# Three experts with 64 slots and two products per weight tile, placed by token count

## What is computed

```python
def moe_swiglu(h, router, w_gate, w_up, w_down):
    probs = softmax(ht @ router)                    # 256 tokens x 8 experts
    vals, idx = top_k(probs, 2); wts = vals / sum(vals)
    gates = ...                                     # token x expert, two non-zero per token
    for e in range(8):
        out = out + gates[:, e:e + 1] * swiglu(ht, w_gate[e], w_up[e], w_down[e])
# swiglu(h) = (silu(h @ w_gate) * (h @ w_up)) @ w_down; 1024 -> 2048 -> 1024
```

## Time and profile before

| | us |
|---|---|
| median of 3 runs | 1329.01 |
| lowest, highest | 1328.97, 1330.6 |
| span of the profiled execution | 1327.3 |
| TensorE busy in it | 1291.5 (97%) |
| TensorE weight loads | 1074.6 (81%) |
| VectorE busy | 931.9 (70%) |
| ScalarE busy | 835.5 (63%) |
| moved by DMA | 341.68 MB, 257 GB/s |

### The profile page before, as it was taken

One profiled execution on the slowest core, in us unless ns is written; L12 is line 12 of the kernel. 1 busy time (PEld: TensorE's weight loads), 2 busy tenths in 40 slices (PEclk: granted clock), 3 DMA queues, 4 the chain that ended last, 5 costly groups with the idle time before them and its releaser, 6 DMA issues.

```text
span 1327.3 us, 16327 instructions
## 1 busy us (share of the span) xinstructions
PE 1291.5 (97%) x6201; PEld 1074.6 (81%) x6201; DVE 931.9 (70%) x906; ACT 835.5 (63%) x906; POOL 49.6 (4%) x52
## 2 busy tenths in 40 slices
PE   7999999999999999999999999999999998999998
PEld 6888888888887888888888888878778876788887
DVE  4685555446768888888888888898876664645542
ACT  5646444346866878777787878877587655644431
POOL 4001000000005000000000000002010000000000
PEclk9999999999999999999999999999999999999999
DMA  9647755544228999999999999999864341555540
GB/s 313 235 142 271 245 177 172 181 147 149 80 95 323 422 377 414 346 422 358 408 353 410 359 408 365 396 378 380 318 224 167 118 159 64 189 187 174 180 159 32
DMA packets 90233, 341.68 MB, mean 257 GB/s; under 512 B 6267, under 2 KB 14160, under 8 KB 66512
## 3 DMA queue, kind: packets, MB, share of 16 engines
q1 hardware_dynamic: 87200, 330.15, 66.6%
q0 software_dynamic: 2816, 10.67, 2.3%
q10 hardware_dynamic: 160, 0.07, 0.0%
HBM read 333.53 MB, written 11.01 MB: 260 GB/s over the span
## 4 chain that ended last, share of the span: by engine, by line
PE 92%; DVE 4%; ACT 3%; issue 1%; DMA 0%; ACTq 0%; DVEq 0%
PE bank L1704 29%; PE bank L1706 28%; PE bank L1705 28%; DVE w_lo L365 1%; PE bank L2056 1%; PE bank L1816 1%; PE bank L1799 1%; PE bank L1843 1%; ACT w_hi L360 1%; PE bank L2049 0%; DVE x L1076 0%; PE bank L1989 0%; ACT mem_tmp L651 0%; ACT xT_hi L594 0%; DMA gain_rows<-in_norm_mix 0%
## 5 line engine op out<-in xcount | busy, mean ns | idle before, releaser
L365 DVE TENSOR_TENSOR w_lo<-raw,w_hi 128x2048 fp32r<-128x2048 f32 (+3 forms) x246 | 549.3, 2246 | 223.5 <-ACT w_hi L360 222.5
L360 ACT ACTIVATE w_hi<-raw 128x2048 fp32r<-128x2048 f32 (+3 forms) x246 | 460.9, 1883 | 209.6 <-PE bank L1706 197.9
L1704 PE MATMUL bank<-w_hi,xT_hi 128*128 128x512 f32 (+2 forms) x672 | 256.5, 382 | 3.8 <-DVE xT_lo L1048 1.9
L1706 PE MATMUL bank<-w_hi,xT_lo 128*128 128x512 f32 (+2 forms) x672 | 253.4, 377 | 0.0
L1705 PE MATMUL bank<-w_lo,xT_hi 128*128 128x512 f32 (+2 forms) x672 | 253.3, 377 | 0.0
L1704 PE MATMUL bank<-w_hi,gT_hi 128*128 128x512 f32 x512 | 201.5, 394 | 2.8 <-DVE gT_lo L1520 1.5
L1706 PE MATMUL bank<-w_hi,gT_lo 128*128 128x512 f32 x512 | 200.2, 391 | 0.0
L1705 PE MATMUL bank<-w_lo,gT_hi 128*128 128x512 f32 x512 | 199.8, 390 | 0.0
L365 DVE TENSOR_TENSOR w_lo<-raw_beside,w_hi 128x2048 fp32r<-128x2048 f32 x64 | 145.3, 2288 | 8.5 <-ACT w_hi L360 8.4
L1704 PEld LDWEIGHTS bank<-w_hi,xT_hi 128*128 128x128 f32 x672 | 126.8, 189 | 27.8 <-issue 3.7
L360 ACT ACTIVATE w_hi<-raw_beside 128x2048 fp32r<-128x2048 f32 x64 | 122.1, 1917 | 39.5 <-PE bank L1706 38.4
(11 more groups left out here) (381 smaller groups left out, 1340.7 us busy)
## 6 DMA issues: line engine op xcount, KB each, us to landing
raw<-in_moe_w_gate SPq DMA_DIRECT2D x48, 1024.0 KB, 6.0
raw<-in_moe_w_up SPq DMA_DIRECT2D x48, 1024.0 KB, 7.3
raw_beside<-in_moe_w_down SPq DMA_DIRECT2D x32, 1024.0 KB, 9.3
raw<-in_moe_w_down SPq DMA_DIRECT2D x32, 1024.0 KB, 7.7
raw<-in_w_gate_up SPq DMA_DIRECT2D x22, 1024.0 KB, 5.1
raw_beside<-in_moe_w_gate SPq DMA_DIRECT2D x16, 1024.0 KB, 6.5
raw_beside<-in_moe_w_up SPq DMA_DIRECT2D x16, 1024.0 KB, 6.1
raw<-in_ffn_w_gate SPq DMA_DIRECT2D x11, 1024.0 KB, 5.2
```

Source lines behind the costliest of these rows:

```text
L360: nc.scalar.activation(w_hi[:, slot, :n], raw_of(i, stream)[:, :n], ACT.Copy).then_inc(stream.high, 1)
L365: nc.vector.tensor_tensor(w_lo[:, slot, :n], raw_of(i, stream)[:, :n], w_hi[:, slot, :n].bitcast(F32), ALU.subtract).then_inc(stream.low, 1)
L1704: mm(dst, a_hi, b_hi, start=start, stop=False)
L1706: return mm(dst, a_lo, b_hi, start=False, stop=stop)
```

## The change

Experts 1 to 7 are run in an order by their token count: with the counts ranked, places 2, 4 and 6 go to the three lightest, places 1, 3, 5 and 7 to the others; expert 0 stays first. VectorE computes places, first slots and the order in `positions`, inside the first expert, behind low part 3, and `rows_of_choices` comes behind low part 4 instead of ahead of the first expert. SyncE's loop over experts is written out, and it reads the expert of each place from `order` into a register, by which the weights are addressed.

A light place has 64 slots. The high parts of its 64 rows and their low parts stand side by side as the 128 columns of one stationary tile, so one weight tile needs two products, by its high and by its low part (`both`). The two halves of a result have to be added. For gate and up TensorE does it and turns at the same time: ScalarE copies the bank to memory, and a plain float32 product with the constant `fold` (128x64) gives the sum, transposed (`fold_quarter`); silu and the product by up follow on the folded data. For down VectorE adds the halves. More than 64 tokens in a light place, or 128 in another, lead to the second pass.

The other experts keep three products. In the loop, the first two chunks of a gate now start with banks 2 and 3 for both chunks, ahead of the wait for `y`. One loop body now holds two experts.

```diff
+                def both(dst, tokens, wh, wl, start, stop):
+                    mm(dst, tokens, wh, start=start, stop=False)
+                    return mm(dst, tokens, wl, start=False, stop=stop)
+                def fold_quarter(v, b, quarter):
+                    columns = columns_of(v, quarter, 2)
+                    for k in range(4):
+                        at_ = (quarter % 2 * 4 + k) * LIGHT
+                        ins = mm(bank[b][:, at_:at_ + LIGHT], columns[:, k // 2, k % 2, :], fold, start=True, stop=True)
+                    return ins
```

VectorE, light expert and first expert:

```diff
+                def light(e, i, n_high):
+                    for c in range(EXPERT_CHUNKS):
+                        if c == 15:
+                            light_product(e, i, 0)
+                            light_low(e, 0)
+                        split_low(MOE0 + c + AHEAD, e, W1)
+                        if c == 15:
+                            light_product(e, i, 1)
+                        if c == 16:
+                            light_low(e, 1)
+                        if c in (17, 18):
+                            rows_low(n_high + c - 17, 6 + c - 17, c - 17)
+                    dve.wait_ge(sem("light_copied"), y_copied(i))
+                    dve.wait_ge(sem("moe_rows_stored"), 16 + 16 * e)
+                    for half in range(2):
+                        cols = slice(half * HALF, (half + 1) * HALF)
+                        ins = V.tensor_tensor(M["y"][:LIGHT, cols], bank[half][:LIGHT, :], y_low[:, cols], ALU.add)
+                    ins.then_inc(sem("moe_y"), 1)
+                def expert(e, h, n_high, rows_low, first=False):
                     for c in range(EXPERT_CHUNKS):
                         if c == 14:
+                            expert_act(e, h, 0)
                         split_low(MOE0 + c + AHEAD, e, W1)
+                        if first and c == 0:
+                            positions()
+                        if first and c == 1:
+                            rows_of_choices()
...
                 below_best()
-                rows_of_choices()
                 dve.wait_ge(sem("loaded_moe_g"), 16)
```

ScalarE, light expert:

```diff
+                def light(e, i, number):
+                    for c in range(EXPERT_CHUNKS):
+                        split_high(MOE0 + c + AHEAD, e, W1)
+                        if c in (8, 9):
+                            light_gate(e, number, 2 * (c - 8))
+                            light_gate(e, number, 2 * (c - 8) + 1)
+                        if c == 14:
+                            light_silu(i)
+                            for quarter in range(QUARTERS):
+                                light_up(e, i, quarter)
+                        if c in (15, 16):
+                            light_high(e, c - 15)
+                        if c in (17, 18):
+                            rows_high(number + c - 17, 6 + c - 17, c - 17)
```

TensorE, the gate of an expert in the loop, and the middle of a light one:

```diff
+                def gate(e, product, y_read):
+                    first_two = [(k, weights(W1, MOE0 + k, e)) for k in range(2)]
+                    for quarter in (2, 3):
+                        for k, (wh, wl) in first_two:
+                            product(quarter, k, wh, wl, quarter)
+                    pe.wait_ge(sem("moe_y"), y_read)
...
+                def light(e, i, number):
...
+                    pe.wait_ge(sem("light_copied"), gate_copied(i))
+                    for quarter in range(QUARTERS):
+                        ins = fold_quarter(M["e_act"], 2 + quarter // 2, quarter)
+                    ins.then_inc(sem("light_in_psum"), 1)
+                    last_two = [(k, weights(W1, MOE0 + KD + k, e)) for k in (KD - 2, KD - 1)]
```

SyncE:

```diff
+                for p in range(E):
+                    if p == 1:
+                        sp.wait_ge(sem("moe_planned"), 2)
+                    e = sp.value_load(order[0:1, p:p + 1], min_val=0, max_val=E - 1) if p else 0
                     for c in range(EXPERT_CHUNKS):
+                        load_expert(c, p, p == 0, *expert_chunk(A, e, c, p == E - 1))
                         if c == 13:
+                            store_rows(p)
+                        if c == 14 and p < E - 1:
+                            load_rows(p + 1)
```

More of the change, by code:

```diff
@@ L416, in returned, with over_job, over_heavy, heavy_of_pair @@
             return M["back"][:, at, :] if at < 2 * T - 1 else M["moe_g"][:, :]
[L418 to L422, removed]
-            return FIRST_OVER - OVER_JOBS * E + OVER_JOBS * e
+        def over_job(e):
+            return FIRST_OVER - OVER_JOBS * E + OVER_JOBS * e
+        def over_heavy(e):
+            return e - PAIRS
+        def heavy_of_pair(i):
+            return 1 + 2 * i, 1 + i, FIRST_PAIR + PAIR_JOBS * i
+        def light_of_pair(i):
+            return 2 + 2 * i, FIRST_PAIR + TURNED_JOBS + PAIR_JOBS * i
+        SLOTS_AT = [LIGHT if 0 < p < E - 1 and p % 2 == 0 else P for p in range(E)]
+        FIRST_SLOT = [sum(SLOTS_AT[:p]) for p in range(E)]
+        def gate_copied(i):
+            return QUARTERS + 9 * i
+        def up_copied(i, quarter):
+            return QUARTERS + 1 + quarter + 9 * i
+        def y_copied(i):
+            return 9 + 9 * i
+        def gate_turned(i):
+            return 1 + 6 * i
+        def light_up_done(i, quarter):
+            return 2 + quarter + 6 * i
+        def up_turned(i, j):
+            return 5 + j + 6 * i
+        def gated(e, j):
+            return 1 + j + QUARTERS * e
+        def act_high(e, j):
+            return 3 + j + QUARTERS * e
+        def act_known(e, j):
+            return 1 + 2 * j + QUARTERS * e
+        def act_low(e, j):
+            return 2 + 2 * j + QUARTERS * e
         def per_feature(c, n):
@@ L531, in _ @@
                 pool.wait_ge(W1.high, start_of["ffn1_up"] + 4)
-                for e in range(1, E):
-                    small(slots_in[e * P:(e + 1) * P, :], A["shape_blank"], "blank")
+                for p in range(1, E):
+                    at_, n = FIRST_SLOT[p], SLOTS_AT[p]
+                    small(slots_in[at_:at_ + n, :], A["shape_blank"][:n, :], "blank")
                 pool.wait_ge(sem("mla_heads_ready"), 1)
@@ L2086, in expert, with first_expert @@
+                def expert(e, h, number):
+                    pe.wait_ge(sem("moe_drained"), number)
+                    gate(e, product, 1 + e)
+                    pe.wait_ge(sem("moe_act_done"), QUARTERS * e)
+                    rest_of_expert(e, h, number)
+                def first_expert():
+                    pe.wait_ge(sem("moe_drained"), GATHER_JOBS - 1)
                     for k in range(KD):
-                        if first and k == KD // 2:
-                            pe.wait_ge(sem("moe_drained"), number)
```

303 lines of the change are left out of this document (215 added, 88 removed).

## The result

The changed kernel takes 1338.99 us (1337.59 to 1341.67) against 1329.8 (1328.97 to 1331.05) for the kernel before in the same measurement: a ratio of 1.0065, 95% interval 1.0044 to 1.0086. It is slower, by 0.65%. 1314.8 was forecast, over 1303 to 1330. The profiled span is 1335.4 us against 1327.3.

A forecast was written before the change was run, and what follows sets the result against it. TensorE was taken to bound the kernel, with VectorE 8.5 us behind per expert and setting the pace of the lights. The sum was 1329.0 - 20.8 (lights) + 0.8 + 5.8 (first expert) = 1314.8 us, range 1303 to 1330.

The forecast's parts named there:

- first expert: Earlier first product, 1.3 us less, against late low parts 4 and 5: net +0.8 us; plus a 5.8 us stall.
- first light and its heavy: A light expert costs 61.0 us instead of 68.4, and the heavy one behind fills the ring again: 7.4 us less.
- third light and last expert: After the third light the last expert waits for the result before any product, starting at 63.7 us: gains 6.0 us.
- The product step: One 128x512 product on TensorE takes 0.2267 us from start to start; 288 products make 65.3 us of an expert.
- Rival C: Slower by the scatter wait alone, if SyncE is released after about 463 us: some 1334 to 1340 us; chance 0.09.
- The lead of the loads: Chunks landed or under way for about 9 us cover a light's transfers: nothing taken, up to 4 us per light.
- The walk: Light expert followed from the preceding heavy expert's last product: VectorE sets the pace, equivalent start of the next at 61.0 us.
- Rival B: Transfers set a light expert's pace, 65 to 68 us; gains 0.4 to 3.4 each, 1325 to 1334 us; chance 0.17.
- "TensorE keeps the whole saving" (D): TensorE stays the bound and three lights save 50 us: 1286 us in all; chance 0.02.
- The scatter stall: First expert: late scatters delay SyncE's load of chunk 15, and TensorE stalls 5.8 us (1.5 to 7.1, up to 12).
- A (hidden): Late scatters finish in 18 us or the ring covers them: 1309 us, and to 1303; chance 0.19.
- any clock loss: TensorE's clock halving after idle: 1 to 2 us more after the first expert's stall; left out there and in lights.

The follow-up runs named there:

- after_64: The changed kernel with its stage tiles moved back 32 bytes onto a multiple of 128 bytes; 1329.45 us, ratio 0.9986 to the kernel before.
- after_64_half_loads: after_64 with only half of each weight chunk loaded in the three light places; 1321.65 us, ratio 0.9936 to the kernel before.
- after_64_rows_17: after_64 with SyncE's load of the next expert's rows behind weight chunk 17 instead of 14; 1320.58 us, ratio 0.9934 to the kernel before.
- after_64_best: after_64_rows_17 with three orders changed: first gate products by chunk, the last expert started likewise, a light's result added ahead of low part 26; 1310.32 us, ratio 0.9866.
- before_late_rows: The kernel before with only the rows of the choices moved behind low part 5 of the first expert; 1335.37 us, ratio 1.0047.

## Why the prediction was wrong, point by point

The span of after_64 is 1326.4 where the sum, less the 1.7 us beside the span, gives 1313.1, and that of after is 1335.4. Differences from the kernel before, in us, from the ends of the experts (before: 480.11, 548.52, 685.37, 822.22, 955.14):

| step | forecast | after_64 | after |
|---|---|---|---|
| first expert | +6.6 | +7.5 | +10.5 |
| expert 1 | 0 | -0.1 | +1.6 |
| first light and its heavy | -7.4 | -3.6 | -3.2 |
| second light and its heavy | -7.4 | -3.4 | -1.3 |
| third light and last expert | -6.0 | -2.0 | -1.1 |
| behind it | 0 | +0.7 | +1.6 |
| sum | -14.2 | -0.9 | +8.1 |

**The product step, the error that turned the sign.** "0.2267 us from start to start" was carried over to a kernel whose stationary tiles lie elsewhere. The step of the mixture's products is 0.2333 in after. It accounts for the 9.0 us between the last two columns: 1.8 us are lost before the first expert's first product (410.30 against 408.48, the feed-forward ahead), and most of the rest in the first and the heavy experts, which TensorE binds. The diff shows the new tile and the longer constants; the prediction listed what was added to the queues, not what was added to memory. None of the rivals had it. Rival C gave "some 1334 to 1340", which holds the 1338.99, but by luck: its reason was a stall of over 15 us in the first expert, and there were 4.8. A forecast without this error would still have been off by 14 us: after_64's 1329.45 lies at the upper edge of the 1303 to 1330, and the 14.2 us that were to be saved are not there.

**The lead of the loads, the second error.** "This lead lasts almost to its end. I take nothing, with up to 4 us per light." With the row load where it was, a light of after_64 took 60.8, 61.9 and 60.2; with loads out of the way 58.6. The walk itself was right to about 1 us: in after_64_half_loads low part 3 ends 5.2 us behind the start, as forecast, low part 17 at 36.0 (36.2), the first low part of the activation at 40.8 (40.1), and VectorE idles 4.8 us (4.2). So the loads cost 2.2, 3.3 and 1.6 us a light, 7 in all, within the bound of 4 each that I had given and not in the sum. Up to the end of the last expert half_loads is 6.6 us shorter than after_64, of the 11.8 that are missing in the three rows with a light. Rival B had the wait right (high parts waiting for loads: 17.0 us in after, the first expert's stall among them) and the price too high. It took all 26 MB at 383 to 400 GB/s, 65 to 68 us. The rate was that, 394 to 402 in the lights of after_64, but a part of the bytes had landed before a light began: 401 GB/s over 60.8 us are 24.4 MB. What the walk left out was that a store and a row load stand ahead of just those chunks which the folds and the activation need at once. Two rows of after's list of waits:

```profile
ACT w_hi L370 <- DMA raw<-in_moe_w_up: 17.0, 8, 3.5
...
PEld bank L2257 <- DVE w_lo L375: 27.4, 48, 1.3
```

The second row confirms the other half: in the lights TensorE's loads of stationary tiles wait for VectorE's low parts, 48 times. VectorE sets the pace there. The folds were a little dearer than the 7.0 us of the sum, 3.87 + 3.98 = 7.9 in the first light of after_64, and "TensorE keeps the whole saving" (D) was out of the question.

The Trainium skill (DMA: Bandwidth & Descriptors, Specifications) gives about 358 GB/s, half of a stack's 716, as the limit of one core; by it a light expert would take 73 us, an estimate. The first in after took 60.5 at 399 GB/s, so this trace, with one core at work, does not bear that figure out as a limit.

**The heavy expert behind a light.** Forecast: low part 23 ends at 55.8 in the walk, so the light's last product at 57.6; the next heavy expert waits 2.6 us for its second chunk and 0.8 for the result, which makes 71.8 from end to end. After_64 has 72.5 and 71.6, after_64_rows_17 71.5. Right, and after_64_best shows that 2.0 of it were avoidable.

**The first expert.** The scatter stall was the forecast's best step: TensorE was to stall 5.8 us and lost 4.8 (5.4 in after_64). SyncE was to be released at 446 and was at 446.03, which is closer than the working was: the scatters began 1.3 us later than forecast, behind slower products, and took 20.5 us instead of 21.8. In after_64 the release is at 444.40. `before_late_rows` shows it alone. Rivals A (hidden) and C (over 15 us) fall. The waits for low parts 4 and 5 came out at 2.3 + 1.0 us in after_64 against 2.1. That the whole comes so near, +7.5 against +6.6, is partly luck, since two clock terms that the sum left out nearly cancel: behind the stall the granted clock of after_64 is 0.55 over 3.3 us, about 1.5 us lost, and at the first products it is 1.00 where before had 0.88 over 14 us, about 1.7 us gained.

**The last expert.** The wait for the result was forecast (57.6 to 63.7 in the walk, 6.1 us), and 5.7 are there. "I leave it out of the sum, as I do any clock loss" is what failed: the first products behind the gap are

```profile
895.27 0.76 PE L1885 MATMUL bank<-w_hi,gT_hi 128*128 128x512 f32 x1 [5.70 <-DVE y L1604]
895.84 0.63 PE L1886 MATMUL bank<-w_lo,gT_hi 128*128 128x512 f32 x1
896.26 0.63 PE L1887 MATMUL bank<-w_hi,gT_lo 128*128 128x512 f32 x1
```

The last two starts are 0.42 apart, the 1.2 GHz level. Behind a gap of 5.7 instead of 1.3 us the last expert should take some 64.5 + 4.5 = 69.0 us to its first half result; in after_64 it takes 70.7 and in after_64_rows_17 71.2, so the clock costs about 1.7 to 2.2. The granted clock agrees: 0.50 over the 3.6 us from 888.4 in after_64, 1.8 us lost. In after_64_best the gap is gone and with it the fall.

**Open.** The 1.6 us of after behind the mixture were not broken down; the second feed-forward uses moved stationary tiles for 264 products there, which at 0.0066 us each would make 1.7, but after_64 has 0.7 there without them. Of the 11.8 us that the rows with a light fall short in after_64, the loads explain 6.6 and the last expert's clock about 2; the other 3 are about 1 per light, 58.6 in half_loads against the 57.6 of the walk, and were not split further. Why either operand's start matters on a scale of 128 bytes was not found out.

## What to carry to other kernels

When an edit adds a tile, write down on which bytes every TensorE operand then starts, and pad to a multiple of 128; a comparison of two kernels whose tiles lie differently compares that too. When an engine is relieved, price each queue by what stands ahead of the few transfers that a serial chain waits for, and not only by its mean rate. And a wait that leaves TensorE idle costs more than its length where the granted clock falls behind it.

## What the runs showed of the hardware that was not expected

- A 128x512 fp32r product whose stationary tile starts 32 or 64 bytes off a multiple of 128 steps at 0.2333 us instead of 0.2267 (2.9% more), and one whose moving tile starts 32 off at 0.2344 (3.4%), at a granted clock of 1.00. Chunk-wide operations of VectorE and ScalarE on the same shifted tiles keep their durations.
- With half of TensorE's weight products taken away in the lights, a light took longer: 63.8 us instead of 60.8, at a granted clock of 0.71 over 576 to 626. TensorE was busy for 38.1 of these 50 us, in short pieces.
- Four indirect scatters of 0.5 MB each, issued beside a full queue of weight loads, take 20.2 to 20.7 us from first issue to release. In before it is 27.7, because two of the four issues hold GpSimd for 4.1 and 9.8 us instead of about 1.9; from the end of the last issue to the release it is 9.6 us there and 10.9 to 11.4 in the others.
